# A second ring for the expert weights: odd expert pairs use the dense weights' buffers, and the expert loop takes two pairs per turn

## What is computed

```python
def second_block(x, ...):
    h = x
    for i in range(DEPTH):                     # 2
        hn = rms_norm(h, norm_mix[i])
        ...                                    # i = 0: forgetting attention, i = 1: retention
        hn = rms_norm(h, norm_ffn[i])
        h = h + hier_moe(hn, ...)
    return rms_norm(h, norm_final)

def expert_block(args):
    xb, e = args
    a, b = jnp.split(xb @ w_gu[e], 2, axis=-1)   # w_gu[e]: 1024 x 1024
    return (jax.nn.silu(a) * b) @ w_down[e]      # w_down[e]: 512 x 1024
```

## Time and profile before

| | before |
|---|---|
| runs | 2138.66 us median of 3 (2137.78 to 2138.73) |
| profiled execution | span 2133.2 us; its own time isn't listed apart |
| instructions | 32348 |
| PE busy | 1998.2 us, 94% |
| DVE, ACT busy | 915.6 us, 711.7 us |
| read from HBM | 601.27 MB |
| chain that ended last | PE 62%, DMA 28%, DVE 4%, ACT 3%, issue 2% |
| experts of layer 0 | first silu 954.11 us, last 1391.34 us |
| experts of layer 1 | first silu 1670.40 us, last 2106.69 us |

### The profile page before, as it was taken

One profiled execution on the slowest core, in us unless ns is written; L12 is line 12 of the kernel. 1 busy time (PEld: TensorE's weight loads), 2 busy tenths in 40 slices (PEclk: granted clock), 3 DMA queues, 4 the chain that ended last, 5 costly groups with the idle time before them and its releaser, 6 DMA issues.

```text
span 2133.2 us, 32348 instructions
## 1 busy us (share of the span) xinstructions
PE 1998.2 (94%) x12788; PEld 1448.0 (68%) x12789; DVE 915.6 (43%) x1524; ACT 711.7 (33%) x1111; POOL 80.3 (4%) x119
## 2 busy tenths in 40 slices
PE   7898999999999998889999999989998999999997
PEld 5876899988999897754444444479898444344443
DVE  4876678755644444442222121246555222222212
ACT  3435365243653355621111111144453111111112
POOL 0110211100100200000000000000000000000000
PEclk8998999999999999989999999999999999999999
DMA  9740388912655342479999999935266899999996
GB/s 358 276 145 30 131 305 325 343 64 80 237 179 187 108 141 98 198 311 395 422 423 422 422 422 421 422 138 192 81 214 269 346 422 422 422 422 422 422 422 262
DMA packets 108256, 603.71 MB, mean 283 GB/s; under 512 B 10094, under 2 KB 10548, under 8 KB 59012
## 3 DMA queue, kind: packets, MB, share of 16 engines
q1 hardware_dynamic: 96016, 559.91, 66.5%
q0 software_dynamic: 11872, 42.35, 5.5%
q10 hardware_dynamic: 276, 0.13, 0.0%
HBM read 601.27 MB, written 1.05 MB: 282 GB/s over the span
## 4 chain that ended last, share of the span: by engine, by line
PE 62%; DMA 28%; DVE 4%; ACT 3%; issue 2%; SPq 0%; ACTq 0%; DVEq 0%
DMA expert_w<-in_expert_w_gu 25%; PE bank L977 11%; PE bank L573 10%; PE bank L575 10%; PE bank L574 10%; PE bank L989 4%; PE bank L607 3%; PE bank L962 3%; PE bank L582 1%; PE bank L584 1%; PE bank L583 1%; DMA dense_w<-in_mlp_w 1%; ACT w_high L432 1%; DMA dense_w<-in_w_in 1%; DVE w_low L439 1%
## 5 line engine op out<-in xcount | busy, mean ns | idle before, releaser
L977 PE MATMUL bank<-expert_w,work 128*64 128x512 f32 (+1 forms) x2240 | 457.8, 597 | 46.7 <-DMA expert_w<-in_expert_w_gu 46.4
L977 PEld LDWEIGHTS bank<-expert_w,work 128*64 128x64 f32 (+1 forms) x2240 | 152.0, 133 | 346.5 <-issue 346.3
L439 DVE TENSOR_TENSOR w_low<-dense_w,w_high 128x2048 fp32r<-128x2048 f32 x112 | 255.9, 2290 | 217.0 <-ACT w_high L432 216.4
L432 ACT ACTIVATE w_high<-dense_w 128x2048 fp32r<-128x2048 f32 x120 | 228.6, 1910 | 313.3 <-DMA dense_w<-in_mlp_w 191.1
L989 PE MATMUL bank<-expert_w,work 128*64 128x512 f32 (+1 forms) x1120 | 226.8, 595 | 0.0
L2157 DVE TENSOR_TENSOR work<-work,bank 128x512 f32<-128x512 f32 x32 | 22.0, 688 | 385.2 <-ACT work L1457 385.2
L989 PEld LDWEIGHTS bank<-expert_w,work 128*64 128x64 f32 (+1 forms) x1120 | 70.0, 132 | 136.4 <-issue 134.2
L1457 ACT ACTIVATE work<-bank 128x512 f32<-128x512 f32 x32 | 19.1, 597 | 421.9 <-PE bank L977 421.9
L573 PE MATMUL bank<-u_pairs_mlp,w_high 128*128 128x256 f32 x512 | 144.1, 284 | 2.0 <-issue 1.1
L573 PE MATMUL bank<-hidden_pairs,w_high 128*128 128x256 f32 x512 | 145.0, 283 | 0.0
L575 PE MATMUL bank<-hidden_pairs,w_high 128*128 128x256 f32 x512 | 145.0, 283 | 0.0
(11 more groups left out here) (399 smaller groups left out, 3856.3 us busy)
## 6 DMA issues: line engine op xcount, KB each, us to landing
expert_w<-in_expert_w_gu SPq DMA_DIRECT2D x256, 1024.0 KB, 23.0
expert_w<-in_expert_w_down SPq DMA_DIRECT2D x128, 1024.0 KB, 19.2
dense_w<-in_mlp_w SPq DMA_DIRECT2D x64, 1024.0 KB, 5.5
dense_w<-in_ret_w_in SPq DMA_DIRECT2D x24, 1024.0 KB, 5.3
u<-in_ada_w POOLq DMA_DIRECT2D x40, 512.0 KB, 7.0
work<-in_ada_w POOLq DMA_DIRECT2D x40, 512.0 KB, 6.8
dense_w<-in_fox_w_in SPq DMA_DIRECT2D x16, 1024.0 KB, 5.1
dense_w<-in_w_in SPq DMA_DIRECT2D x12, 1024.0 KB, 7.3
```

Source lines behind the costliest of these rows:

```text
L432: nc.scalar.activation(HIGH_OF[at], dense_w[:, at % RING], ACT.Copy, scale=scale).then_inc(S("w_high_ready"), 1)
L439: ins = nc.vector.tensor_tensor(w_low[:, at % RING], dense_w[:, at % RING], high, ALU.subtract)
L977: last = mm(free[half][cols, :], rows[:, k, cols], pieces[:, k // 2, a, k % 2, half * 512:(half + 1) * 512], start=k == 0, stop=k == KT - 1)
```

## The change

- The pieces j = 0 and 1 of every odd pair go to the four buffers of the dense ring, all others stay where they were (`piece_of`). The waits of SP and PE follow: those pieces are counted on the dense ring's semaphores, and SP may load them once the pair before last has used them.
- Pair 1 is loaded without a look at `swap`, its j = 0 and 1 right behind pair 0. So `few` is the second expert's count in pair 1 too.
- PE's loop, and SP's, take two pairs per turn, an even and an odd one. PE's last two pairs are written out behind the loop; the very last has no gather and adds up before it turns the hidden values. ACT's and DVE's last pair is written out too, without what the gather needs.
- In layer 0 the retention's first four chunks are loaded behind the last pair, each once the piece in its buffer has been used; in layer 1 the gain row likewise. Pieces 3 and 4 of layer 0's pair 0 go out when the attention's last scores have been made.

```diff
+        def piece_of(odd, j, a):
+
+            return dense_w[:, 2 * j + a] if odd and j < RING // 2 else pieces[:, j, a]
...
-            eng.wait_ge(dense_in[at % RING], 16 * (at // RING + 1))
+            eng.wait_ge(dense_in[at % RING], 16 * (at // RING + 1 + (PAIRS // 2 if at >= chunk("ret_in", 0, 0) else 0)))
...
+            for x in range(2):
+                wait_tile(sp, TILES["fox_attn"] + fox_tile(FOX_HEADS // 2 - 1, x))
+            for j in (3, 4):
+                load_experts(0, 0, j)
             for l in range(DEPTH):
 
                 wait_tile(sp, TILES["ret_out" if l else "fox_out"] + 7)
-                for j in range(3 if l == 0 else 4, PIECES // 2):
+                for j in range(4 if l else 5, PIECES // 2):
                     load_experts(l, 0, j)
+                for j in range(RING // 2):
+                    load_experts(l, 1, j, 1)
+                for j in range(RING // 2, PIECES // 2):
+                    sp.wait_ge(expert_used, PIECES * PAIRS * l + 2 * j + 2)
+                    load_experts(l, 1, j, 1)
+                sp.wait_ge(S(f"more_known_{l}"), 1)
+                with sp.Fori(1, PAIRS // 2) as two:
+                    for odd in range(2):
+                        i = 2 * two + odd
+                        swap = sp.value_load(more_i[0:1, ds(i + 3 * PAIRS, 1)], min_val=0, max_val=1)
+                        for j in range(PIECES // 2):
+                            before = 2 if j < RING // 2 else 1
+                            sp.wait_ge(expert_used, PIECES * (PAIRS * l + i - before) + 2 * j + 2)
+                            load_experts(l, i, j, odd, swap)
+                last = PIECES * (PAIRS * (l + 1) - 1)
+                if l == DEPTH - 1:
+                    sp.wait_ge(expert_used, last + 2)
+                    sp.dma_start(gain_row, ...)
                 if l == 0:
                     for j in range(RING):
+                        sp.wait_ge(expert_used, last + 2 * (j // 2) + 2)
                         load(chunk("ret_in", 0, j))
-                if l == DEPTH - 1:
-                    sp.dma_start(gain_row, ...)
-                sp.wait_ge(S(f"more_known_{l}"), 1)
-                with sp.Fori(1, PAIRS) as i:
-                    swap = sp.value_load(more_i[0:1, ds(i + 3 * PAIRS, 1)], min_val=0, max_val=1)
-                    for j in range(PIECES // 2):
-                        sp.wait_ge(expert_used, PIECES * (PAIRS * l + i - 1) + 2 * j + 2)
-                        load_experts(l, i, j, swap)
...
-                with pe.Fori(0, PAIRS) as i:
+                def one_pair(i, two, odd, last=False):
...
+                    if last:
+                        pending(count)
+                        add_up().then_inc(S("added"), 1)
+                        pe.wait_ge(S("hidden_e"), n + 1)
+                        turn_hidden(S("hidden_turned"))
+                        pe.wait_ge(S("pick_w_ready"), n + 1)
+                        turn_pick(pick_w, S("pick_turned"))
+                        pe.wait_ge(S("hidT_ready"), n + 1)
+                    else:
...
+                with pe.Fori(0, PAIRS // 2 - 1) as two:
+                    for odd in range(2):
+                        one_pair(2 * two + odd, two, odd)
+                for odd in range(2):
+                    one_pair(PAIRS - 2 + odd, PAIRS // 2 - 1, odd, last=odd == 1)
...
-                with act.Fori(0, PAIRS) as i:
+                with act.Fori(0, PAIRS - 1) as i:
+                    one_pair(i)
+                one_pair(PAIRS - 1, last=True)
...
-                V.tensor_copy(few[:, 0:1], counts[:, 1, 0:1])
-                V.tensor_tensor(few[:, 1:PAIRS], counts[:, 0, 1:PAIRS], counts[:, 1, 1:PAIRS], ALU.min)
+                V.tensor_copy(few[:, 0:2], counts[:, 1, 0:2])
+                V.tensor_tensor(few[:, 2:PAIRS], counts[:, 0, 2:PAIRS], counts[:, 1, 2:PAIRS], ALU.min)
```

More of the change, by code:

```diff
@@ L967, in experts, with project @@
                             LARGE: [(slice(UNIT * x, UNIT * (x + 1)), int(x == 3)) for x in range(4)]}
-                def project(rows, loaded, used=None, first=SLOTS, late=None):
+                def project(rows, two, odd, used=None, first=SLOTS, late=None):
                     for k in range(KT):
@@ L973, in project @@
                             pe.wait_ge(S("xg_dve"), late)
-                        both_in(k, loaded)
+                        both_in(k, two, odd)
                         for half in range(2):
                             for cols, a in tiles_of[first]:
-                                last = mm(free[half][cols, :], rows[:, k, cols], pieces[:, k // 2, a, k % 2, half * 512:(half + 1) * 512],
+                                last = mm(free[half][cols, :], rows[:, k, cols], piece_of(odd, k // 2, a)[:, k % 2, half * 512:(half + 1) * 512],
                                           start=k == 0, stop=k == KT - 1)
@@ L981, in project, with down @@
                     return last
-                def down(loaded, used=None, first=SLOTS):
+                def down(two, odd, used=None, first=SLOTS):
                     for f in range(4):
-                        both_in(KT + f, loaded)
+                        both_in(KT + f, two, odd)
                         for half in range(2):
@@ L1067, in experts @@
                         with pe.If(first_rows == first):
-                            project(xg, loaded, expert_used, first, late=count)
-                    pe.wait_ge(S("pick_ready"), count + 1)
-                    pending(count)
-                    for half in range(2):
-                        gather(half, pick).then_inc(S("gathered"), 1)
-                    pe.wait_ge(S("hidden_e"), n + 1)
-                    turn_hidden(S("hidden_turned"))
-                    pe.wait_ge(S("pick_w_ready"), count)
@@ L1077, in experts @@
-                    turn_pick(pick_w, S("pick_turned"))
-                    add_up().then_inc(S("added"), 1)
-                    pe.wait_ge(S("hidT_ready"), n + 1)
-                    pe.wait_ge(S("xg_act"), count + 1)
-                    pe.wait_ge(S("xg_dve"), count + 1)
+                            project(xg, two, odd, expert_used, first, late=n + 1)
+                    if last:
[6 more added lines that the diff above has]
+                        pe.wait_ge(S("hidT_ready"), n + 1)
+                    else:
+                        pe.wait_ge(S("pick_ready"), n + 2)
+                        pending(count)
+                        for half in range(2):
+                            gather(half, pick).then_inc(S("gathered"), 1)
+                        pe.wait_ge(S("hidden_e"), n + 1)
+                        turn_hidden(S("hidden_turned"))
+                        pe.wait_ge(S("pick_w_ready"), n + 1)
+                        turn_pick(pick_w, S("pick_turned"))
+                        add_up().then_inc(S("added"), 1)
+                        pe.wait_ge(S("hidT_ready"), n + 1)
+                        pe.wait_ge(S("xg_act"), n + 2)
+                        pe.wait_ge(S("xg_dve"), n + 2)
@@ L1082, in experts @@
                     for first in (SLOTS, LARGE):
                         with pe.If(first_rows == first):
-                            down(loaded, expert_used, first)
+                            down(two, odd, expert_used, first)
+                with pe.Fori(0, PAIRS // 2 - 1) as two:
[3 more added lines that the diff above has]
+                    one_pair(PAIRS - 2 + odd, PAIRS // 2 - 1, odd, last=odd == 1)
```

65 lines of the change are left out of this document (39 added, 26 removed).

## The result

| | before | after |
|---|---|---|
| runs | 2138.69 us median of 4 (2137.78 to 2142.36) | 2243.49 us median of 4 (2240.35 to 2250.44) |
| profiled execution | span 2133.2 us | span 2243.1 us, its own time 2244.93 |
| layer 0, first to last silu | 437.23 us | 500.83 us |
| layer 1, first to last silu | 436.30 us | 485.17 us |

The change makes the kernel slower: the ratio is 1.0486, with a 95% interval from 1.0466 to 1.0506. The forecast was 2146 with a range up to 2185, so even the range missed it. The spans differ by 109.9 us. Of these 63.6 lie in layer 0's pairs and 48.9 in layer 1's; 3.0 came ahead of the first silu (954.11 before, 957.11 after; in other runs of these kernels it came anywhere from 949.8 to 957.8), and what follows the last silu of each layer is 1.6 and 4.0 us shorter.

What follows compares the result with a forecast made beforehand. PE was taken to bound the first pairs, expert transfers the later ones. From the 2138.66 us median, -5.6 (tail), +7.7 and +2.9 (code past the transfers) and +2 (transfers held back) made +7.0: forecast 2146 us, range 2131.5 to 2185.

Steps and rivals of the forecast that it cites:

- the price of a return: PE's two-pair loop, jumping back to its start: 5.0 us each, bounds 0 and 6.4, six returns a layer.
- What is fetched: PE's loop code: each return fetches two blocks, the one returned to and the one past the further rounds.
- rival B: PE's loop: every block falls out in each turn, with waits in odd copies too; 2182 us, chance 0.22.
- The small terms of the code: PE's first turns, 3 us in layer 0 and 1.5 in layer 1, and 1.5 for pair 14.
- The sum: Whole kernel: -5.6 tail, +7.7 and +2.9 code past the transfers, +2 transfers held back, +7.0 us in all.
- PE's hand: Time PE alone would reach each layer's last silu earlier: 26.8 us in layer 0, 30.1 in layer 1.
- The preload at nothing: Loading 4 MB of pair 1 earlier: gains nothing because SP issues in order; bounds 0 and 9.9 us a layer.
- Rival C: Expert transfers: the preload pays in full, 19.9 us, if SP's order was misread; 2113 us, chance 0.03.
- The tail: Last pair without a gather, projection to down projection: 2.8 us less per layer, 5.6 in all, bounds 0 to 3.6.
- The retention's weights late: Retention's first weights queued behind pair 15: costs nothing, with 2 us to spare.
- the `few` change: Pair 1's packing: matters only if packed 96 to 32, which pair 1 never is; nothing.

Runs made afterwards that it cites:

- a third of the load: The changed kernel with every expert transfer from pair 2 on cut to a quarter of its columns; 2185.12 us, one run.
- two-pair loop alone: The kernel before, with nothing changed but PE's loop, which holds two pairs per turn; 2298.85 us, ratio 1.0741.
- 1800 instructions: The changed kernel with PE's block for further rounds in the even copy alone; 2225.91 us, ratio 1.0405.
- 1500 instructions: The changed kernel without PE's block for further token rounds, which these inputs never run; 2134.67 us, ratio 0.9974.
- The one copy: The changed kernel's rings and SP order, but the loops of before on PE, ACT and DVE, only the projection's first half standing twice; 2133.33 us, repeated 2135.13.
- the last order: The one copy, with SP issuing as buffers come free up to pair 7 and in order of use from pair 8; 2128.65 us, ratio 0.9957.

## Why the prediction was wrong

**The step that failed is the price of a return.** Where PE stands was foreseen: the loop doesn't stay, PE stands for the block returned to and for the one that the jump over the further rounds lands in, and the clock falls after it. But 5.0 us was taken, with 6.4 as the bound. Measured over PE's own pace, the six returns of layer 0 cost 81.7 us and those of layer 1 72.7: 12.9 each in the mean, 12.0 in ten of them and 17.0 in the two to pairs 8 and 10. The bound was 2 x 3.2 us from the one wait for code that the trace of before had the earlier trace rows: 3.2 us is the step to pair 1 of 30.36 us less PE's pace of 27.15, with a granted clock of 0.86 over 955 to 960 us. That row couldn't carry the bound, for two reasons that the runs show. First, a part of that fetch lay beside work already issued: its packet started at 953.60 us, PE had work until 954.54 and went on at 956.03, so 0.94 us at least were covered, and more if the fetch was asked for at the jump of 949.62, which isn't shown. A return fetches twice in a row, and the second time PE has nothing left in issue: 3.3 and 3.8 us of waits, with 1.9 us of register instructions bare between them, and a projection that is 3.1 us longer at the lower clock. Second, the returns fall among full DMA queues, which adds 3.8 us to each in layer 1; at a third of the load a return costs 8.3 us there, still over the bound.

**What is fetched.** Forecast: the two blocks at either end of the loop. Measured: all, about ten packets a turn, so rival B was right on the packets (over 190, and 213 came). But B's waits within the odd copies didn't come in the changed kernel: there the branches past the rounds and past the 96-row form take 1.3 to 4.0 us, and PE has as much issued. In the two-pair loop alone they did come (0.7 to 2.2 us). Why there and not here stays open; B's own reason, where a block ends, may decide it. It is an estimate from the one wait of before, where PE worked 0.48 us (three matmuls of the gather) behind the jump before it stood 1.49; no run shows where the blocks end.

How many instructions stay, and which blocks are lost first, no run shows. The forecast supposed that the last blocks overwrite only the first ones, 94 packets and 48 more; the 187 packets at 1800 instructions and the 213 at 2100 speak against it. The loops of 1340 and 1500 instructions stay (72 and 83 packets), and between 1500 and 1800 no run places the limit. The return to pair 12 that cost nothing at 1800 isn't explained.

**The small terms of the code.** Forecast 3, 1.5 and twice 1.5 us for first turns and pair 14, 7.5 in all. Measured: nothing in the first turn (27.14 us to pair 1, where the kernel before took 30.36), but at pairs 14 and 15 together 4.4 us in layer 0 and 6.0 in layer 1, and 7.3 at pair 11 of layer 0: 17.7 in all. Pair 11 is one of the three packed 96 to 32; the other two are pairs 8 and 10, and the returns to them are the dearest, steps of 44.08 and 44.21 us. The forecast hadn't priced the code of the 96-row form: PE stands 5.37 us in front of pair 11's projection (the jump there took 5.59), and 3.22 and 3.28 us inside those of pairs 8 and 10.

**The sum.** Code was priced at 34.5 + 33.0 = 67.5 us and cost 93.6 + 79.0 = 172.6. These 105.1 us are the whole miss of 97.5, within 8 us. PE's hand of 26.8 and 30.1 us agrees with the layers (in layer 1 79.0 - 30.1 is the 48.9 us lost; in layer 0 the first turn's 3.2 us come to it), and was gone after three returns.

**The preload at nothing: right for this order.** SP's issue of pair 1's j = 4 stands at 967.08 us after a share of 0.45, as the earlier trace rows had 967.43 after 0.47. The one copy, which waits for no code inside the two layers, has them 2 to 3 us shorter, of a bound of 9.9; in layer 0 that is about the first turn's code wait, which didn't come, and in layer 1 the 2.0 to 2.3 us are what the preload may have brought. The reason given held, too: it is the order of issue that wastes the lead, as the 426.91 us of the last order show. Rival C had the size right for layer 1 and the kernel wrong.

**The tail: right, then spent.** From projection to down projection 3.57 us (3.6 was forecast) and 3.50 in layer 1; the retention's first split starts 17.09 us after the last silu instead of 20.00, 2.9 us less. But code behind the loop has to be fetched, and pairs 14 and 15 paid for it; alone, the last pair brings nothing that its interval shows (ratio 1.0004, 0.9985 to 1.0023). The forecast's lower bound of 0 is what came.

**The retention's weights late, and the `few` change: right, nothing.** The first split starts at 1475.03, as soon as ACT has made its way to it, and waits for no transfer; pair 1 has the 64-row form.

## What to carry to other kernels

Count a loop's code before unrolling it, with the blocks that are jumped over: on TensorE 1500 instructions in a loop cost nothing here and 1800 cost 12 us a turn, and the same two rings fit in some 1340 by writing twice only what differs. A wait read from a trace is what was left of a fetch after the work that ran beside it; ask what the same fetch costs where two come in a row with nothing issued ahead and the DMA engines full. A second buffer for a part of the pieces gives a lead only in that part, and it becomes time only when the order of issue is changed while both sides still have work left.

## What was not expected of the hardware

- The loop's branch to code that is gone took 7.28 us in the median among full DMA queues and 4.84 at a third of the load. The same jump took 6.23 or 3.35 us, waited for 2.16 us or not at all, with the weights' transfers begun 6.2 us earlier or not. The packets took 0.9 to 2.3 us in each case; what grew was the time before the first one started, 3.1 or 3.9 us instead of 0.5 or 1.0.
- Six hundred instructions that are never executed cost 105 us: they made the loop too long to stay. Yet a loop of 1800 stayed for one turn, behind the turn that ran the 96-row form twice.
- With BRANCH_PREFETCH_HINT at the head of the turn the loop's branch took 5.59 us instead of 7.28, and the next one 3.9 as before. One packet came in it where two came without the hint, and nowhere in the turn was there one more.
- Two programs with the same two-pair loop, 2100 instructions, lost in other places: one at returns alone, the other in odd copies too (layer 0 at 500.83 and 531.27 us).
